# Modulation in four wide pairs with four products interleaved, its later two thirds moved beside w_pw and w_out, and GpSimd taken out of the first stage

## The chip, the cores and the metric

The kernel runs on one core of one Trainium2 chip. The metric is device time in microseconds (us), the median of three runs. Engines are named as in the profile: PE is TensorE (PEld its weight loads), DVE is VectorE, ACT is ScalarE, POOL is GpSimd and SP is SyncE, which issues all of the kernel's DMAs here.

## What is computed

Two transformer blocks on 512 tokens of width 1024, in float32. Only the first half of the first block matters here:

```python
mod = jnp.einsum("bd,de->be", jax.nn.silu(c), w_ada[l]) + b_ada[l]
sh1, sc1, g1, sh2, sc2, g2 = jnp.split(mod[:, None, :], N_MOD, axis=-1)
h = rms_norm(x, norm_mix_g[l]) * (1.0 + sc1) + sh1
proj = jnp.einsum("bsd,de->bse", h, w_in[l]) + b_in[l]
...
a = glu_in[..., :CONV_WIDTH] * jax.nn.sigmoid(glu_in[..., CONV_WIDTH:])
a = causal_depthwise_conv(a, conv_dw_w[l], conv_dw_b[l])
a = jax.nn.silu(layer_norm(a, conv_ln_g[l], conv_ln_b[l]))
y_conv = jnp.einsum("bsc,cd->bsd", a, w_conv_pw[l]) + b_conv_pw[l]
...
y = jnp.einsum("bsd,de->bse", g_conv * y_conv + g_mlstm * y_mlstm, w_out[l])
x = x + g1 * y
h = rms_norm(x, norm_ffn_g[l]) * (1.0 + sc2) + sh2
...
x = x + g2 * jnp.einsum("bsf,fd->bsd", jax.nn.silu(gt) * up, w_ffn_down[l])
```

The depthwise convolution has 31 taps per channel. `w_ada` is 1024 by 6144: 24 MB of weights for one vector times matrix. Of its six outputs the first two (`sh1`, `sc1`) are wanted before the first projection, `g1` first after `w_out`, `sh2` and `sc2` before the feed-forward, `g2` after it.

## The kernel before

Activations lie transposed, channels on the partitions: eight tiles of 128 channels by 512 tokens. A projection works by output tiles of 128 channels, with eight k tiles of 128. Each weight and each activation is cut into a high and a low part, and one k tile costs three products of 128x128 by 128x512: weight high and weight low times activation high (L1295, L1296), weight high times activation low (L1303). An output tile is so 24 products.

`plan()` writes one list of steps; each engine then runs, in that order, the part of each step that is its own. So a step that is added stands in the same place in every engine's queue, and an engine that waits holds back all that stands behind it.

Weight tiles come in over SP into a ring of four raw buffers (`load`). `split` makes the high part on ACT (L1446) and the low part on the engine `lo_engine` (POOL, L2245, until the convolution gate; DVE, L1694, after it) into a ring of three. `W["ahead"]` says how many units are cut in advance of the one that is finished.

Spare DVE work is handed out between products: `between()` is called three times per output tile, and `rate` says how many items of `spare` go into DVE's queue each time. In the opening six chunks of `w_ada`, 1 MB each and 256 outputs wide, are loaded. For the first eight chunks DVE takes five of the eight k tiles (`mod_near`, L1724, L1728), ACT three (`mod_far`, L1466) and POOL adds these (L2256, L2258); PE sums over the partitions with a column of ones (L1336), and DVE and ACT make the normed and shifted activations (`mod_tiles`), while two output tiles are interleaved k by k (`gemms`). The other sixteen chunks are 128 DVE items (`ada`, L1769, L1773) handed out in the GLU projection, at 3 per call. Behind them come the taps of the convolution: seven channel tiles on DVE (`tap`, L1791, L1794), pairs of tiles alternating, and the eighth on POOL (`tap_far`, L2270 to L2276).

The order of the work around the change is: the GLU projection (16 output tiles), `w_v` (two blocks of 96 products, in four banks at once), the gates `w_if`, q and k of four heads (16 tiles, each with three taps of a short convolution on DVE, L1860), each head's attention as side work (`attend`: scores L1363, values L1371, transposes L1377), 16 gate tiles, then `conv_sum(7)` and its product L1382, the 8 tiles of the convolution gate with the layer norm beside them, `w_pw`, `w_out`, and the first feed-forward. `w_pw` has three DVE operations per tile (L1920, L1923, L1925, with ACT's L1557 between the last two), `w_out` has one and a sum (L1930, L1700).

Of the kernel before, what the change touches and what calls it, by code (L numbers as in the profile page):

```python
# [7 lines left out]
ALU = mybir.AluOpType  # L8
# [32 lines left out]
GMIX, GFFN = 8, 80  # L41
SCALE = 1.0 / float(np.sqrt(96.0))
# [57 lines left out]
def plan():  # L100
# [25 lines left out]
    W = {"cut": 0, "used": 0, "finished": 0, "ahead": 2, "loaded": 0}  # L126
    lo_engine = ["pool"]
# [27 lines left out]
    far, side, spare, later_ops = [], [], [], []  # L155
    rate, due, tick = [0, 0, 0], [0.0, 0.0], [0]
# [17 lines left out]
    def between():  # L174
        while later_ops and later_ops[0][0] <= tick[0]:
            later_ops.pop(0)[1]()
        tick[0] += 1
        step(rate[0])
        due[0] += rate[1]
        background(int(due[0]))  # L180
        due[0] -= int(due[0])
        due[1] += rate[2]
        while due[1] >= 1:
            due[1] -= 1
            if far:
                far.pop(0)()
# [48 lines left out]
    def gemms(jobs, acts, together=2, hook=None, feed=None):  # L235
# [15 lines left out]
        ready("dve")  # L251
# [107 lines left out]
    order = [0, 4, 1, 5, 2, 6, 3, 7] + list(range(8, 24))  # L359
    place = {ch: n for n, ch in enumerate(order)}  # L360

    def ada_load(n, after=()):
        add("ada_load", n, order[n], after)

    for n in range(6):
        ada_load(n)
    for _ in range(NRAW - 1):
        load()
    csil = keepc(8)
    add("csil", csil)  # L370
    ss, other = SumSq("x0a"), SumSq("x0b")
    for i in range(8):
        if i % 2:
            other.add(("XT", i), [("x", 0, i)], eng="pool")
        else:
            ss.add(("XT", i), [("x", 0, i)])
    add("merge", ss.a, other.a, ss.t, other.t)
    tmp.give(other.a, ("merged",))
    ss.t = ("merged",)
    b0 = rows_of(ss, D)  # L380
    mod_a, mod_b, mod_c = misc.take(), misc.take(), misc.take()
    turns, turn_free = [mod_a[0], mod_c[0]], [mod_a[1], mod_c[1]]
    gmix = keepc(8)

    def mod_sums(p):
        chs, accs = (p, p + 4), [tmp.take(), tmp.take()]
        more = []
        for z, ch in enumerate(chs):
            more.append(tmp.take())
            add("mod_far", ch, place[ch] % 6, more[z], accs[z])  # L390
        for k in range(5):
            for z, ch in enumerate(chs):
                add("mod_near", ch, place[ch] % 6, k, accs[z])
        for z, ch in enumerate(chs):
            add("mod_sum", ch, accs[z][0], more[z][0], turns[p % 2], turn_free[p % 2])
            tmp.give(more[z][0], ("mod_sum", ch))
            tmp.give(accs[z][0], ("mod_cols", ch))
            ada_load(place[ch] + 6, [("mod_sum", ch)])

    def mod_tiles(p):  # L400
        add("mod_tiles", p, turns[p % 2])
        turn_free[p % 2] = [("mod", p)]

    mod_sums(0)
    add("xn", b0)
    misc.give(b0, ("xn", 7))
    mod_sums(1)
    load()

    def mod_feed(k):  # L410
# [11 lines left out]
    ada_acc = {}

    def ada_part(ch, k):
        if k == 0:
            ada_acc[ch] = tmp.take()
        add("ada", ch, place[ch] % 6, k, ada_acc[ch])
        if k == 7 and place[ch] + 6 < 24:
            ada_load(place[ch] + 6, [("ada", ch, 7)])
# [16 lines left out]
    def glu(i):  # L446
# [14 lines left out]
        def then():  # L461
            if i % 2:
                taps.extend(sums)
                sums.clear()
                if i < 7:
                    sums.append(lambda: conv_sum(i))
                taps.extend([lambda z=z, j=j: add("tap", i - 1 + z, j)
                             for j in range(31) for z in range(2) if i - 1 + z < 7])
# [3 lines left out]
    taps, sums, waiting = [], [], []  # L472
    for ch in range(8, 24, 2):
        parts = [lambda k=k, c=c: ada_part(c, k) for k in range(8) for c in (ch, ch + 1)]
        spare.extend(parts[:6] + waiting + parts[6:])
        waiting = [lambda ch=ch: (ada_columns(ch), ada_columns(ch + 1))]
    rate[:] = [0, 3, 0]
    gemms([job for i in range(8) for job in glu(i)], "n1", feed=mod_feed)
    background(1000)
    spare.extend(taps)  # L480
    far.extend([lambda j=j: add("tap_far", j) for j in range(31)])

    def last_columns():
        yield
        ada_columns(22)
        ada_columns(23)
        add("modb", mod_b[0])
        misc.give(mod_b[0], ("modb",))

    side.append(last_columns())  # L490
    rate[:] = [1, 3.5, 0.3]

# [100 lines left out]
    rate[:] = [1, 1.35, 0.3]  # L593
# [19 lines left out]
    rate[:] = [1, 1.6, 0.3]  # L613
    for n, (first, i) in enumerate([(32, i) for i in range(6)] + [(48, i) for i in range(6)] +
                                   [(32, 6), (32, 7), (48, 6), (48, 7)]):
        if n == 8:
            rate[1] = 2.1
# [4 lines left out]
    while far:  # L622
        far.pop(0)()
# [34 lines left out]
    rate[:] = [1, 0, 0]  # L658
    lo_engine[0] = "dve"
# [16 lines left out]
    gemms([("w_pw", i, pw_evac(i), None) for i in range(8)], "a")  # L676
    rate[:] = [0, 0, 0]
# [9 lines left out]
    gemms([("w_out", i, out_evac(i), None) for i in range(8)], "z", 0)  # L687
# [5 lines left out]
    def ffn_up(which, acts, names, hook=None):  # L693
# [100 lines left out]
    rate[:] = [1, 0, 0]  # L794
# [270 lines left out]
def program(nc, A, out, known):  # L1065
    steps, units = plan()
    ctx = ExitStack()
    with ctx:
# [27 lines left out]
        TRIG = place("trig", o, [128, 4, S]); o += 4128  # L1096
        HT = place("htok", o, [128, 4, 258]); o += 4128
# [15 lines left out]
        ADA = [place(f"ada{i}", B + 33728 + 8192 * i, [128, 8, 256]) for i in range(6)]  # L1113
# [32 lines left out]
        XN = CO  # L1146
# [71 lines left out]
        def _(e):  # L1218
# [59 lines left out]
            run({"begin": begin, "load": load, "ada_load": ada_load, "v_begin": v_begin, "rot_load": rot_load,  # L1278
# [4 lines left out]
        def _(e):  # L1283
# [1173 lines left out]
```

## Time and profile before

| | us |
|---|---|
| median of 3 runs | 1799.83 (1798.41 to 1801.11) |
| the profiled execution | 1799.9 |
| its span, first to last instruction | 1797.8 |
| PE busy in the span | 1623.5 |
| DVE busy | 1100.4 |
| ACT busy | 641.2 |
| POOL busy | 413.9 |

Busy shares are means over stages with different limits: PE is busy in 90% of the span, DVE in 61%, but DVE in nearly all of the first 540 us. 2.1 us of the execution lie outside the span. Starts in the rows are in us from the span's start; some records of matmuls are missing from the trace.

### The profile page before, as it was taken

Reading aid. Unit: us, or ns where it says so; the run is one execution under the profiler, and the core shown is the slowest. Engines: PE = TensorE matmul, PEld = TensorE weight load, DVE = VectorE, ACT = ScalarE, POOL = GpSimd, SP = SyncE. Lnnn points to the kernel's source line nnn. Section 1 sums busy time; section 2 is a strip of 40 time slices with the busy share of each in tenths; the row PEclk is TensorE's granted clock in tenths of the full one; section 3 lists DMA queues with packets and bytes.
Section 4 is the critical chain, followed back from the end, with each engine's and each line's share of the span. In section 5 each row is a group of like instructions: output and inputs, shape, how many; then the busy total and the mean of one; then the engine's idle time right before and its main releaser. Section 6 shows DMA issues by size and latency. Waiting matters only on the chain.

```text
span 1797.8 us, 18431 instructions
## 1 busy us (share of the span) xinstructions
PE 1623.5 (90%) x7112; PEld 1310.5 (73%) x7112; DVE 1100.4 (61%) x1538; ACT 641.2 (36%) x917; POOL 413.9 (23%) x242
## 2 busy tenths in 40 slices
PE   2898768778857998999999999899997999999988
PEld 2787656556746787888888888677885888888876
DVE  6889798899995455333337344866647444443246
ACT  4321135554416334223223322344634322322223
POOL 4445654556731001000001100100024111110010
PEclk9899889889988998999999999999999999999999
DMA  8672211111222332333333332221132333333332
GB/s 327 233 278 97 59 47 48 47 55 51 68 61 59 95 105 71 94 100 99 94 94 97 89 114 73 69 69 49 36 117 94 94 96 104 94 88 97 97 117 70
DMA packets 44734, 172.86 MB, mean 96 GB/s; under 512 B 4964, under 2 KB 5092, under 8 KB 41320
## 3 DMA queue, kind: packets, MB, share of 16 engines
q1 hardware_dynamic: 44648, 171.69, 30.2%
q8 instruction: 56, 0.92, 0.2%
q14 instruction: 30, 0.25, 0.0%
HBM read 167.48 MB, written 4.19 MB: 95 GB/s over the span
## 4 chain that ended last, share of the span: by engine, by line
PE 63%; DVE 13%; ACT 3%; issue 2%; POOL 0%; DVEq 0%; ACTq 0%; POOLq 0%
PE bank L1295 19%; PE bank L1296 19%; PE bank L1303 19%; DVE convout L1794 5%; PE bank L1388 1%; PE bank L1401 1%; DVE hm L1906 1%; PE bank L1331 1%; DVE XT L2183 1%; DVE tmp L1860 1%; PE bank L1315 1%; DVE spl L1694 0%; PE bank L1317 0%; DVE tmp L2180 0%; PE bank L1316 0%
## 5 line engine op out<-in xcount | busy, mean ns | idle before, releaser
L1295 PE MATMUL bank<-HH,sph 128*128 128x512 f32 x1496 | 608.9, 407 | 17.0 <-ACT HH L1665 5.2
L1296 PE MATMUL bank<-HH,spl 128*128 128x512 f32 x1496 | 594.9, 398 | 0.0
L1694 DVE TENSOR_TENSOR spl<-raw,sph 128x1024 fp32r<-128x1024 f32 (+1 forms) x207 | 265.6, 1286 | 334.4 <-ACT sph L1446 334.2
L1303 PE MATMUL bank<-HL,sph 128*128 128x512 f32 x1496 | 392.3, 398 | 1.1 <-DVE HL L2187 1.1
L1446 ACT ACTIVATE sph<-raw 128x1024 fp32r<-128x1024 f32 (+1 forms) x263 | 271.4, 1034 | 241.9 <-PE bank L1303 173.8
L1295 PEld LDWEIGHTS bank<-HH,sph 128*128 128x128 f32 x1496 | 289.0, 193 | 88.0 <-issue 16.4
L1296 PEld LDWEIGHTS bank<-HH,spl 128*128 128x128 f32 x1496 | 288.9, 193 | 62.0 <-issue 2.2
L1303 PEld LDWEIGHTS bank<-HL,sph 128*128 128x128 f32 x1496 | 284.3, 191 | 65.2 <-DVE HL L2187 2.9
L1794 DVE SCALAR_TENSOR_TENSOR convout<-convin,vecs,convout 128x512 f32<-128x512 f32 x210 | 215.5, 1074 | 0.9
L2245 POOL TENSOR_TENSOR spl<-raw,sph 128x1024 fp32r<-128x1024 f32 x56 | 165.2, 2954 | 175.3 <-ACT sph L1446 175.3
L2251 POOL TENSOR_TENSOR tmp<-tmp,tmp 128x512 f32<-128x512 f32 x44 | 60.1, 1372 | 555.4 <-ACT tmp L1454 554.7
L1295 PE MATMUL bank<-midh,sph 128*128 128x512 f32 x352 | 138.7, 394 | 0.0
L1296 PE MATMUL bank<-midh,spl 128*128 128x512 f32 x352 | 138.7, 394 | 0.0
L1585 ACT ACTIVATE midh<-tmp 128x512 fp32r<-128x512 f32 x44 | 27.8, 632 | 192.9 <-DVE tmp L1975 97.8
L1303 PE MATMUL bank<-midl,sph 128*128 128x512 f32 x352 | 89.9, 394 | 0.0
L1303 PEld LDWEIGHTS bank<-midl,sph 128*128 128x128 f32 x352 | 65.8, 187 | 16.3
L1295 PEld LDWEIGHTS bank<-midh,sph 128*128 128x128 f32 x352 | 65.8, 187 | 16.3
L1296 PEld LDWEIGHTS bank<-midh,spl 128*128 128x128 f32 x352 | 65.8, 187 | 16.3
L2305 POOL TENSOR_TENSOR midl<-tmp,midh 128x512 fp32r<-128x512 f32 x22 | 28.4, 1293 | 206.9 <-ACT midh L1585 206.9
L1773 DVE SCALAR_TENSOR_TENSOR tmp<-ada,kept,tmp 128x256 f32<-128x256 f32 x112 | 67.8, 673 | 0.0
L1860 DVE SCALAR_TENSOR_TENSOR tmp<-xpad,vecs,tmp 128x512 f32<-128x512 f32 x48 | 57.5, 1198 | 3.3 <-ACT tmp L1504 2.0
L2274 POOL TENSOR_SCALAR rrow<-convin,vecs 128x512 f32<-128x512 f32 x30 | 59.0, 1967 | 0.0
(287 smaller groups left out, 1707.6 us busy)
## 6 DMA issues: line engine op xcount, KB each, us to landing
raw<-in_w_in SPq DMA_DIRECT2D x73, 512.0 KB, 3.6
raw<-in_w_up SPq DMA_DIRECT2D x66, 512.0 KB, 3.6
ada<-in_w_ada SPq DMA_DIRECT2D x24, 1024.0 KB, 7.5
raw<-in_w_down SPq DMA_DIRECT2D x32, 512.0 KB, 3.5
raw<-in_w_gate SPq DMA_DIRECT2D x22, 512.0 KB, 3.6
raw<-in_w_down SPq DMA_DIRECT2D x16, 384.0 KB, 3.1
raw<-in_w_v SPq DMA_DIRECT2D x8, 512.0 KB, 3.7
raw<-in_w_pw SPq DMA_DIRECT2D x8, 512.0 KB, 3.6
```

The costliest lines, as they stand in the source:

```text
L1295: e.matmul(P_[b][:], sph(n)[:, q], hi[:, k, :], start=k == 0, stop=False)
L1296: e.matmul(P_[b][:], spl(n)[:, q], hi[:, k, :], start=False, stop=False)
L1303: m = e.matmul(P_[b][:], sph(n)[:, q], low[:, k, :], start=False, stop=last and k == kb - 1)
L1446: e.activation(sph(n), raw(n), ACT.Copy).then_inc(*up("s_w_high", ("wh", n)))
L1694: e.tensor_tensor(spl(n), raw(n), sph(n).bitcast(F32), ALU.subtract).then_inc(*up("s_w_low", ("wl", n)))
L1773: e.scalar_tensor_tensor(wide, x[:, k, :], KEEP[:, k:k + 1], wide, ALU.mult, ALU.add).then_inc(*up("s_ada", ("ada", ch, k)))
L1794: ins = e.scalar_tensor_tensor(CO[:, i, :], src, wt, CO[:, i, :], ALU.mult, ALU.add)
L1860: e.scalar_tensor_tensor(TMP[j][:], XP[:, s, k:k + 512], wt, TMP[j][:], ALU.mult, ALU.add).then_inc(*up("s_qk_conv", ("qk_conv", h, z, k)))
L2245: e.tensor_tensor(spl(n), raw(n), sph(n).bitcast(F32), ALU.subtract).then_inc(*up("s_w_low_p", ("wl", n)))
L2251: e.tensor_tensor(TMP[a][:], TMP[a][:], TMP[j][:], ALU.add).then_inc(*up("s_sum_p", ("ss", name, i)))
L2274: e.tensor_scalar(RROW[:], src, wt, None, ALU.mult).then_inc(*up("s_conv_p", ("tap_mul", j)))
L2305: e.tensor_tensor(ML[:, i, :], TMP[j][:], MH[:, i, :].bitcast(F32), ALU.subtract).then_inc(*up("s_cut_p", ("lo", "m2", i)))
```

## The change

The opening loads the first third of `w_ada` as four pairs (256 outputs of `sh1` and 256 of `sc1`, 512 wide) of four 512 KB transfers each, all into buffers of their own, with the first four weight tiles between them. For each pair DVE takes six of the eight k tiles in one chain, and PE takes the last two in the same accumulation as the sums over partitions: 12 matmuls per pair. The norm and the cut are now those of the later norms (`norm`, `normlo`), with both low parts on DVE. Four output tiles are interleaved instead of two, with a fourth slot of high and low parts for the opening alone. The later two thirds of `w_ada` come as 32 rows of 128x1024 (512 KB), two buffers, one DVE operation each, two per tile of `w_pw`, two per tile in the first half of `w_out`, one per tile in the first eight of the feed-forward; after every eighth, PE makes eight columns and DVE adds the bias. POOL has no `split`, no sum, no tap in the first stage; all eight channel tiles' taps are DVE's, at new rates. The diff, cut to its core:

```diff
-    W = {"cut": 0, "used": 0, "finished": 0, "ahead": 2, "loaded": 0}
-    lo_engine = ["pool"]
+    W = {"cut": 0, "used": 0, "finished": 0, "ahead": 4, "loaded": 0}
+    lo_engine = ["dve"]
...
-        ready("dve")
+        if together == 2:
+            ready("dve")
...
+    mod_a, mod_b, mod_c = misc.take(), misc.take(), misc.take()
+    for p in range(4):
+        add("ada_load", p)
+        if p < 2:
+            load()
+            load()
...
+    def mod_pair(p):
+        turn = (mod_a[0], mod_c[0])[p % 2]
+        acc = tmp.take()
+        add("mod_sum", p, acc, turn, turn_free[p % 2])
+        tmp.give(acc[0], ("mod_cols", p))
+        add("mod_tiles", p, turn)
         turn_free[p % 2] = [("mod", p)]
+        js = [tmp.take() for _ in range(2)]
+        for z in range(2):
+            add("norm", "n1", 2 * p + z, *js[z], b0, [])
+        for z in range(2):
+            add("normlo", "n1", 2 * p + z, js[z][0])
+            tmp.give(js[z][0], ("hi", "n1", 2 * p + z), ("lo", "n1", 2 * p + z))
+
+    mod_pair(0)
 
     def mod_feed(k):
+        if k in (0, 2, 4):
+            mod_pair(k // 2 + 1)
...
+    def ada_more(count):
+
+        for _ in range(count):
+            u = ada_at[0]
+            ada_at[0] += 1
+            add("ada", u)
+            if u + 2 < 32:
+                add("ada_more", u + 2)
+            if u % 8 == 7:
+                b, free = misc.take()
+                add("ada_columns", u // 8, b, free)
+                misc.give(b, ("modb", u // 8))
...
+                spare.extend([lambda z=z, j=j: add("tap", i - 1 + z, j)
+                             for j in range(31) for z in range(2)])
...
-    rate[:] = [0, 3, 0]
-    gemms([job for i in range(8) for job in glu(i)], "n1", feed=mod_feed)
+    rate[:] = [0, 2]
+    gemms([job for i in range(8) for job in glu(i)], "n1", 4, feed=mod_feed)
...
-    rate[:] = [1, 3.5, 0.3]
+    rate[:] = [1, 2.5]
...
-    rate[:] = [1, 1.35, 0.3]
+    rate[:] = [1, 1.2]
...
-    rate[:] = [1, 1.6, 0.3]
+    rate[:] = [1, 1.65]
...
-    gemms([("w_pw", i, pw_evac(i), None) for i in range(8)], "a")
+    add("ada_more", 0)
+    add("ada_more", 1)
+    gemms([("w_pw", i, pw_evac(i), lambda: ada_more(2)) for i in range(8)], "a")
...
-    gemms([("w_out", i, out_evac(i), None) for i in range(8)], "z", 0)
+    gemms([("w_out", i, out_evac(i), lambda: ada_more(2 if ada_at[0] < 24 else 0)) for i in range(8)], "z", 0)
...
+        if which == 1:
+            jobs = [(*job[:3], lambda: ada_more(1 if ada_at[0] < 32 else 0)) for job in jobs]
...
+            def ada_more(u):
+                if u < 2:
+                    w.wait_ge(*fenced("pw"))
+                else:
+                    w.wait_ge(at("ada", u - 2))
+                e.dma_start(MORE[u % 2][:], A["w_ada2"][u]).then_inc(*up(f"d_more{u % 2}", ("more", u), by=16))
...
+            def mod_sum(p, acc, b, free):
+                w.wait_ge(at("csil"), at("ones"), at("ada_w", p, 3), *each(free))
+                for z in range(4):
+                    et = 2 * p + z % 2 + 8 * (z // 2)
+                    column = P_[b][:, et:et + 1]
+                    for k in (0, 1):
+                        e.matmul(column, ADA[4 * p + 3][:, k, token(z)], KEEP[:, 6 + k:7 + k], start=k == 0, stop=False)
+                    w.wait_ge(at("mod_near", p, 5))
+                    m = e.matmul(column, TMP[acc[0]][:, token(z)], ONES[:, 0:1], start=False, stop=True)
+                m.then_inc(*up("s_column", ("mod_cols", p)))
+
+            def ada_columns(cb, b, free):
+                w.wait_ge(at("ada", 8 * cb + 7), at("ones"), *each(free))
+                for i in range(8):
+                    m = e.matmul(P_[b][:, i:i + 1], ACC[:, token(i)], ONES[:, 0:1], start=True, stop=True)
+                m.then_inc(*up("s_column", ("ada_cols", cb)))
...
+            def ada(u):
+                k, s = u % 8, KEEP[:, u % 8:u % 8 + 1]
+                w.wait_ge(at("more", u))
                 if k == 0:
+                    if u:
+                        w.wait_ge(at("ada_cols", u // 8 - 1))
+                    else:
+                        w.wait_ge(*fenced("pw"))
+                    ins = e.tensor_scalar(ACC[:], MORE[u % 2][:], s, None, ALU.mult)
                 else:
+                    w.wait_ge(at("ada", u - 1))
+                    ins = e.scalar_tensor_tensor(ACC[:], MORE[u % 2][:], s, ACC[:], ALU.mult, ALU.add)
```

## Rows read from the trace of the kernel before

**Rows 1.** The page's chain that ended last, shares by engine
```profile
PE 63%; DVE 13%; ACT 3%; issue 2%; POOL 0%; DVEq 0%; ACTq 0%; POOLq 0%
```

**Rows 2.** Busy time by stretch: PE, PEld, DVE, ACT, POOL, granted clock, DMA share, GB/s
```profile
70.00:152.00 82.00, 81.65 (x388) 68.23 (x387) 77.07 (x131) 19.74 (x23) 39.22 (x13) 1.00 0.62 224
152.00:222.00 70.00, 55.62 (x227) 44.49 (x226) 59.19 (x73) 10.42 (x11) 47.12 (x19) 0.88 0.24 73
222.00:407.00 185.00, 142.21 (x559) 108.26 (x558) 167.60 (x218) 94.31 (x138) 96.65 (x50) 0.88 0.17 50
407.00:521.00 114.00, 103.54 (x439) 82.44 (x437) 107.15 (x127) 48.42 (x69) 79.85 (x37) 0.96 0.24 70
521.00:544.00 23.00, 0.16 (x1) 0.00 (x0) 22.15 (x32) 1.40 (x2) 0.00 (x0) 0.61 0.00 0
```

**Rows 3.** What PE waited for, 152 to 545 us: total, times, longest
```profile
PE bank L1377 <- DVE htok L1901: 24.4, 4, 8.0
PE bank L1382 <- DVE tmp L1805: 22.8, 1, 22.8
PE bank L1351 <- DVE row L1850: 12.8, 1, 12.8
```

**Rows 4.** DVE's groups by shape, 222 to 407 us: busy, mean ns
```profile
L1794 DVE SCALAR_TENSOR_TENSOR convout<-convin,vecs,convout 128x512 f32<-128x512 f32 x72 | 69.2, 1005 | 0.0
L1860 DVE SCALAR_TENSOR_TENSOR tmp<-xpad,vecs,tmp 128x512 f32<-128x512 f32 x48 | 57.5, 1198 | 3.3 <-ACT tmp L1504 2.0
```

**Rows 5.** The taps in 522 to 542 us, where POOL is idle
```profile
L1794 DVE SCALAR_TENSOR_TENSOR convout<-convin,vecs,convout 128x512 f32<-128x512 f32 x24 | 18.0, 751 | 0.7
```

**Rows 6.** DVE's timeline (start, us): alternating taps; short taps; POOL idle
```profile
258.85 2.73 DVE L1794 SCALAR_TENSOR_TENSOR convout<-convin,vecs,convout 128x512 f32<-128x512 f32 x4
...
343.40 2.33 DVE L1860 SCALAR_TENSOR_TENSOR tmp<-xpad,vecs,tmp 128x512 f32<-128x512 f32 x3
```

**Rows 7.** DVE's groups, 150 to 156 us: modulation 256 wide, POOL nearly idle
```profile
L1773 DVE SCALAR_TENSOR_TENSOR tmp<-ada,kept,tmp 128x256 f32<-128x256 f32 x12 | 4.9, 475 | 0.0
```

**Rows 8.** Timeline of the opening: the norm's last DVE step; PE's eight column passes (four matmuls)
```profile
18.78 0.87 DVE L1717 TENSOR_SCALAR tmp<-consts,small 128x128 f32<-128x128 f32 x4
...
57.67 1.20 PE L1336 MATMUL bank<-ones,tmp 128*128 128x1 f32 x8 [2.47 <-DVE tmp L1733]
```

**Rows 9.** ACT's timeline: first operations after certain output tiles
```profile
151.78 0.69 ACT L1476 ACTIVATE tmp<-bank,vecs 128x512 f32<-128x512 f32 x1 [5.22 <-PE bank L1303]
...
228.53 0.69 ACT L1501 ACTIVATE xpad<-bank,vecs 128x512 f32<-128x512 f32 x1
...
407.36 0.69 ACT L1537 ACTIVATE tmp<-bank,vecs 128x512 f32<-128x512 f32 x1
...
721.38 0.60 ACT L1577 ACTIVATE tmp<-bank 128x512 f32<-128x512 f32 x1 [3.13 <-PE bank L1303]
...
732.26 0.60 ACT L1577 ACTIVATE tmp<-bank 128x512 f32<-128x512 f32 x1 [3.14 <-PE bank L1303]
```

**Rows 10.** DVE's timeline in w_pw: the first operation of five tiles
```profile
609.27 0.75 DVE L1920 SCALAR_TENSOR_TENSOR tmp<-bank,vecs,gconv 128x512 f32<-128x512 f32 x1
...
612.05 0.75 DVE L1920 SCALAR_TENSOR_TENSOR tmp<-bank,vecs,gconv 128x512 f32<-128x512 f32 x1
...
619.10 0.74 DVE L1920 SCALAR_TENSOR_TENSOR tmp<-bank,vecs,gconv 128x512 f32<-128x512 f32 x1
...
623.36 0.75 DVE L1920 SCALAR_TENSOR_TENSOR tmp<-bank,vecs,gconv 128x512 f32<-128x512 f32 x1
...
639.68 0.75 DVE L1920 SCALAR_TENSOR_TENSOR tmp<-bank,vecs,gconv 128x512 f32<-128x512 f32 x1 [1.25 <-PE bank L1303]
```

**Rows 11.** Busy time by stretch around one wait of PE, columns as above
```profile
368.30:376.60 8.30, 0.32 (x2) 0.00 (x0) 7.75 (x25) 3.96 (x6) 2.24 (x2) 0.75 0.16 56
376.60:382.70 6.10, 6.09 (x19) 5.12 (x20) 6.03 (x6) 2.04 (x3) 5.52 (x2) 0.50 0.15 32
```

**Rows 12.** The page's DMA issues: KB each, us to landing
```profile
raw<-in_w_pw SPq DMA_DIRECT2D x8, 512.0 KB, 3.6
```

More of the change, by code:

```diff
@@ L358, in plan @@
     add("begin")
[L359 to L369, printed above, removed]
+    mod_a, mod_b, mod_c = misc.take(), misc.take(), misc.take()
[4 more added lines that the diff above has]
+            load()
+    csil, gmix = keepc(8), keepc(8)
@@ L370, in plan @@
     add("csil", csil)
-    ss, other = SumSq("x0a"), SumSq("x0b")
+    ss = SumSq("x0")
     for i in range(8):
[L373 to L379, printed above, removed]
-    b0 = rows_of(ss, D)
-    mod_a, mod_b, mod_c = misc.take(), misc.take(), misc.take()
-    turns, turn_free = [mod_a[0], mod_c[0]], [mod_a[1], mod_c[1]]
@@ L383, in plan @@
[L383 to L398, printed above, removed]
@@ L417, in mod_feed @@
+    mod_pair(0)
+    def mod_feed(k):
+        if k in (0, 2, 4):
+            mod_pair(k // 2 + 1)
         if k == 6:
             W["ahead"] = NSPL
+            misc.give(b0, ("norm", "n1", 7))
             misc.give(mod_a[0], *turn_free[0])
             misc.give(mod_c[0], *turn_free[1])
[L422 to L429, printed above, removed]
@@ L436, in plan @@
+    ada_at = [0]
     total = {}
@@ L462, in then @@
             if i % 2:
-                taps.extend(sums)
+                spare.extend(sums)
                 sums.clear()
@@ L466, in then @@
                     sums.append(lambda: conv_sum(i))
-                taps.extend([lambda z=z, j=j: add("tap", i - 1 + z, j)
-                             for j in range(31) for z in range(2) if i - 1 + z < 7])
+                spare.extend([lambda z=z, j=j: add("tap", i - 1 + z, j)
+                             for j in range(31) for z in range(2)])
         return [("w_in", i, keep, None), ("w_in", 8 + i, evac, then)]
[L472 to L476, printed above, removed]
-    rate[:] = [0, 3, 0]
-    gemms([job for i in range(8) for job in glu(i)], "n1", feed=mod_feed)
[L479 to L490, printed above, removed]
-    rate[:] = [1, 3.5, 0.3]
+    sums = []
+    rate[:] = [0, 2]
+    gemms([job for i in range(8) for job in glu(i)], "n1", 4, feed=mod_feed)
+    rate[:] = [1, 2.5]
     fence("v")
@@ L1112, in program @@
         SEL = place("sel", B + 88064, [4, 4, 128])
-        ADA = [place(f"ada{i}", B + 33728 + 8192 * i, [128, 8, 256]) for i in range(6)]
+        ADA = [place(f"ada{i}", B + 17344 + 4096 * i, [128, 2, 512]) for i in range(16)]
         IR, LF, BR, CR = [place(f"row{i}", B + 50176 + 2048 * i, [4, S]) for i in range(4)]
@@ L1700, in total @@
                     e.tensor_tensor(TMP[a][:], TMP[a][:], TMP[j][:], ALU.add).then_inc(*up("s_sum", ("ss", name, i)))
-            def merge(a, b, after, other):
-                w.wait_ge(at(*after), at(*other))
-                e.tensor_tensor(TMP[a][:], TMP[a][:], TMP[b][:], ALU.add).then_inc(*up("s_sum", ("merged",)))
             def rsqrt(name, src, v, q, r, n, scale, after):
@@ L1781, in glu, with ada_columns @@
+            def ada_columns(cb, b, free):
+                part = slice(16 + 8 * cb, 24 + 8 * cb)
+                w.wait_ge(at("ada_cols", cb), at("vecs"))
+                e.tensor_tensor(MOD[:, part], P_[b][:, 0:8], V_[:, VEC["b_ada"] + 16 + 8 * cb:VEC["b_ada"] + 24 + 8 * cb],
+                                ALU.add).then_inc(*up("s_ada", ("modb", cb)))
             def glu(i, b, g, v, j, free):
```

216 lines of the change are left out of this document (69 added, 147 removed).

## Prediction

> **What bounds the kernel now.** I read the page's chain first: PE sets 63% of the end, DVE 13% [rows 1]. The stretches say where DVE does. From 222 to 407 us (q, k and attention) DVE is busy 167.6 of 185 us, from 407 to 521 (gates) 107.2 of 114, and from 521 to 544 PE stands and DVE is busy 22.2 of 23 [rows 2]. The waits give the reason: PE waits 22.8 us for the sum over the convolution's tiles, because DVE is still busy with taps, and 24.4 and 12.8 us for other DVE results [rows 3]. Next come the durations. Beside POOL a tap takes 1005 ns and a short tap 1198 [rows 4]; with POOL idle a tap takes 751 [rows 5], four that alternate between two tiles take 2.73 us, so one each 0.66, and three short ones 2.33, so 0.78 [rows 6]. So the first 540 us are paced by a DVE that POOL slows, and what follows mostly by PE: a feed-forward pair of tiles takes 732.26 - 721.38 = 10.88 us [rows 9], 5.44 per tile, 0.227 per product.
>
> **The opening and the GLU projection.** Its last gate stands at 151.8 us [rows 9]. Removed: ACT's and POOL's share of the modulation, and POOL's sums. Added: per pair one chain on one engine after the other. Six 512-wide operations at 0.78 (the dependent kind) are 4.4 us with the cheaper first. Then PE's columns: 12 matmuls in two passes each, four of the passes early, leave 20; eight take 1.20 us [rows 8], so 3.0 at full clock and up to twice that. Then two small DVE operations, two norms and two low parts, some 4 us. About 12.5 us per pair, and DVE stands during the columns. With four low parts of weights (1.2 each) after the first pair, and a start near 18 us (the norm's last step ends at 19.65 now [rows 8], after a merge with POOL's sum that goes), the pairs end near 31, 48, 61 and 74 us, and the 96 interleaved products near 83. The four products per k tile fill PE's waits, but the next weights' slots come free only then: ACT's table, two sigmoids and a high part, then DVE's low part hold PE for some 5 us more and cost it clock. Twelve tiles are left. DVE per tile: six taps 4.0, a low part 1.15, half a GLU 0.4, together 5.5, as much as PE's 5.44: 66 us, so about 157. **+5** (0 to +12). The loads cost nothing: they are issued at the start, the second pair's weights some 30 us before use, on an SP that now waits for nobody there. POOL's queue holds nothing more before the layer norm, so nobody waits for it.
>
> **w_v and w_if up to the first q tile**: 228.5 - 151.8 = 76.7 us now [rows 9]. 240 products are 54.4. DVE has 47 taps (31 us), ten low parts (11.5) and the adds (5.4): 48, less than PE. With 4 to 5 for the banks that wait: 59. **-18** (-12 to -21).
>
> **q, k and attention**: 407.4 - 228.5 = 178.8 us [rows 9]. DVE's 167.6 [rows 2] are 72 taps and their starts (73), 48 short taps (57.5) [rows 4] and 37 of the rest. After: 57 taps at 0.66 and the starts (38), short taps at 0.78 (37), the rest without POOL some 30, and 16 low parts that were POOL's (18): 124, plus some 12 in which DVE waits for exponentials. So 136 is the lower bound. PE's own work is 16 tiles (87) and three heads (some 11 each): 120, but it must still wait for DVE at each head's values and transposes, and each wait lets the clock fall. The other bound is nearly no gain, because the low parts now stand behind taps in DVE's queue. I take 38 us per head where it is now some 44, and 41 for the first: 155. **-24** (-8 to -38).
>
> **Gates up to the sum's product**: 407.4 to 544.0, 136.6 us [rows 2, 9]. PE: 16 tiles 87, one head 13, waits 6: 106. DVE: 72 taps 48, 16 low parts 18, 16 products 11, the head 12: 89, so no backlog of taps is left and the 22.8 us go [rows 3]. **-30** (-20 to -35). The new rates hand out 72 + 47 + 57 + 79 = 255 items for 251, so none is left over. Sum so far **-67**.
>
> **The later modulation.** 32 operations, 1024 wide. The trace has 475 ns at 256 [rows 7] and 751 at 512 [rows 5]: 276 more per 256, so an estimate of 1.28 each, 2.6 per pair. The Trainium skill, "VectorE: DVE Perf Modes", section "The TRN2 errata", gives (N + 151)/0.96 ns for a float32 tensor_tensor, 1.22 us here; by that the 24 operations up to w_out would be 1.4 us shorter and the result 1788.
>
> In w_pw a tile's three operations take 612.05 - 609.27 = 2.78 us, with the low part 623.36 - 619.10 = 4.26 [rows 10]. Count from 609.27. DVE: tile 0 to 2.8, two operations (one cheaper) to 4.9, tile 1 to 7.7, 10.3, tile 2 13.1, 15.7, tile 3 with its low part 20.0, 22.6. Only then is the eighth operation done, and PE's columns, which stand in PE's queue before tile 4's products, wait for it. PE has ended tile 3 at 639.68 - 4 x 5.44 = 617.9, which is 8.7: it stands 14 us. Eight column matmuls are 16 passes, 2.4 us [rows 8], 3.6 at a fallen clock: 26.2. Tile 4 takes 5.44 + 2.3, since a stretch after a wait of 8 us ran 6.1 us at 0.50 [rows 11]: 33.9. DVE again, 2.78 or 4.26 plus 2.6 each: 59.9 after tile 7, where PE has stood 9.7 us; columns to 63.5. Before, PE was there at 30.4 [rows 10]. **+33**.
>
> In w_out DVE has 4.26 less one operation (0.69), plus 2.6: 6.2 per tile for four tiles. Tile 0 ends at 71.2, the eighth operation at 94.7, PE stood 7 us, columns to 98.3, four tiles and 2.3 to 122.4. Before, 30.4 + 43.5 = 73.9: 48.5 in all, so **+15** here. In the feed-forward DVE has slack but for the last columns: 3.5 of waiting, 2.4, and 2 of clock, **+8**. The 32 transfers: 512 KB land in 3.6 us [rows 12], and some 4 lie between a buffer's use and its next; hidden, barely. On SP the raw loads stand behind them, but a raw tile is wanted four tiles later. If they come late it is 1 us per tile, +10. Without any loss of clock 12 less. **+56** (44 to 66).
>
> The profiled execution took 1799.9 us, 2.1 more than its span and as much as the median 1799.83. 1799.9 - 67 + 56 = **1789**.
>
> **Rivals.** *The bottom goes out of the waits:* DVE, no longer slowed, is never late for PE between 152 and 545 us, so that the 60 us of waits [rows 3] shrink to a tenth and the clock stays up: 15 more gained than the 67, 82, so 1774. For it: DVE's content falls by a quarter. Against: these waits are chains through ACT and DVE, not only lateness. *Slower:* the low parts in DVE's queue hold PE. DVE's queue is in order, and the low part of a tile stands behind the taps of two tiles and a head's scores, which wait for ACT; POOL had no such queue. If that leaves 6 us in q and k, 18 in the gates, 12 in w_v, with +10 at the opening, 26 are gained for 56: 1830. It decides from the point where the first half gains less than 56. *The clock stays low:* PE fell to 0.50 after a wait of 8 us [rows 11] but stands at 1.00 from 70 to 152, where it is busy throughout [rows 2]. If DVE's pace leaves a small wait in each of the 12 GLU tiles and the clock stays at 1.2 GHz in them, a tile takes 10.2 instead of 5.5: 56 more, 1845. The Trainium skill, "TensorE: Matmul & The Clock Gate", section "HAM oscillation", describes such a loop, where every burst begins cold after its wait. In rows 2 short waits of a tile don't show that, so it has a small chance. *The moved modulation is hidden:* only columns and a few us are paid, 13 instead of 56: 1746. Against it: PE's columns wait for DVE in both queues' order.
>
> **How the numbers follow.** 1789 (own range 1778 to 1800) 0.42, of it 0.29 faster, 0.11 same, 0.02 slower; 1774: 0.22; 1830: 0.24; 1845: 0.05; 1746: 0.07. What a measurement of this kernel can tell from no change is about 0.2%, 3.6 us. Faster 0.29 + 0.22 + 0.07 = 0.58, same 0.11, slower 0.31. A range of 1766 to 1830 leaves out the hidden case, the low clock and a little beyond.
>
> **What would show it.** Right: taps at 0.66 to 0.75 us throughout, no wait of 20 us before the sum's product, that product near 477, and three PE waits of 14, 10 and 7 us before columns in w_pw and w_out, with w_out's end 48 us later after the w_pw group than now. Wrong: PE waits for low parts (L1694's successor) in q and k, a product of the sum after 500, or no waits at the columns.

## The result, and the profile after

The changed kernel takes **1757.3 us** (median of 4 runs, 1756.7 to 1758.6) against 1799.1 (4 runs) for the kernel before: ratio 0.9767, 95% interval 0.975 to 0.9784, so 42 us faster. The forecast was 11 us faster, 1789, and the range ended at 1766. The direction was right; the time lies 9 us below the range. The profiled execution took 1756.8 us, its span is 1755.0, again about 2 less.

The chain of work that ended last, by engine [rows 1]:

```profile
PE 66%; DVE 8%; ACT 4%; issue 1%; DMA 1%; POOL 0%; DVEq 0%; ACTq 0%; POOLq 0%
```

DVE's share falls from 13% to 8%. Where the span is cut as in the prediction, ACT's first operation of each part now starts here (timeline, start in us) [rows 9]:

```profile
149.15 0.69 ACT L1446 ACTIVATE tmp<-bank,vecs 128x512 f32<-128x512 f32 x1 [4.32 <-PE bank L1282]
...
207.94 0.69 ACT L1471 ACTIVATE xpad<-bank,vecs 128x512 f32<-128x512 f32 x1
...
346.29 0.69 ACT L1507 ACTIVATE tmp<-bank,vecs 128x512 f32<-128x512 f32 x1
```

The stretches between those points, with the columns of [rows 2]:

```profile
70.00:149.00 79.00, 75.81 (x327) 62.16 (x327) 65.84 (x91) 18.67 (x21) 0.00 (x0) 0.98 0.29 89
149.00:208.00 59.00, 57.13 (x250) 46.31 (x249) 49.08 (x68) 17.07 (x19) 0.24 (x2) 1.00 0.31 96
208.00:346.00 138.00, 124.38 (x530) 95.48 (x529) 119.31 (x218) 87.94 (x130) 0.09 (x1) 0.99 0.22 65
346.00:447.00 101.00, 99.34 (x440) 80.41 (x439) 89.54 (x159) 50.21 (x71) 0.00 (x0) 1.00 0.28 84
```

In q, k and attention DVE has 119.3 us of work where it had 167.6, and the clock of PE is 0.99 where it was 0.88. The gates are PE's: busy 99.3 of 101 us. The stretch in which PE stood for 23 us before the sum's product is gone. DVE's groups by shape in 208 to 346 us [rows 4]:

```profile
L1747 DVE SCALAR_TENSOR_TENSOR convout<-convin,vecs,convout 128x512 f32<-128x512 f32 x59 | 42.3, 744 | 0.0
L1813 DVE SCALAR_TENSOR_TENSOR tmp<-xpad,vecs,tmp 128x512 f32<-128x512 f32 x48 | 36.0, 750 | 2.7 <-ACT tmp L1474 1.4
L1664 DVE TENSOR_TENSOR spl<-raw,sph 128x1024 fp32r<-128x1024 f32 x17 | 20.7, 1218 | 0.0
```

A tap takes 744 ns where it took 1005, a short tap 750 where it took 1198. PE's waits in 149 to 447 us (total, times, longest) [rows 3]:

```profile
PE bank L1274 <- DVE spl L1664: 6.0, 2, 3.6
PE bank L1360 <- DVE htok L1854: 4.8, 3, 1.7
PE bank L1354 <- DVE sc L1824: 2.7, 3, 1.3
PE bank L1334 <- DVE row L1803: 1.1, 1, 1.1
```

The waits for transposes' inputs fall from 24.4 to 4.8 us, the one for the gates' row from 12.8 to 1.1, and the 22.8 for the sum over the convolution is no longer in the list. The new price stands later. PE's largest wait in 440 to 720 us is the one for the accumulator of the moved modulation (`modacc`):

```profile
PE bank L1327 <- DVE modacc L1725: 33.0, 4, 15.2
```

PE's timeline, first around the end of the 96 interleaved products, then around the first columns in `w_pw`:

```profile
78.39 0.40 PE L1282 MATMUL bank<-HL,sph_first 128*128 128x512 f32 x1
81.97 0.47 PE L1274 MATMUL bank<-HH,sph 128*128 128x512 f32 x1 [3.19 <-DVE spl L1664]
...
535.93 3.57 PE L1327 MATMUL bank<-ones,modacc 128*128 128x1 f32 x16 [15.17 <-DVE modacc L1725]
539.37 0.77 PE L1274 MATMUL bank<-ah,sph 128*128 128x512 f32 x1
```

`w_pw` and `w_out` as one stretch, the kernel before in the first fence, the kernel after in the second:

```profile
609.00:683.00 74.00, 74.00 (x324) 60.35 (x322) 42.35 (x51) 21.84 (x28) 0.00 (x0) 1.00 0.33 101
```

```profile
513.00:635.00 122.00, 91.55 (x370) 75.11 (x368) 70.01 (x78) 21.82 (x28) 0.00 (x0) 0.82 0.54 167
```

What took 74 us takes 122: PE stands 30.5 of them, and its busy time is 17.5 longer, at a clock of 0.82. Three groups of columns at 3.57 us, as in the timeline, are 10.7 of that. For the transfers DVE waits only 2.6 us here.

All runs are compared by such stretches. Each is the time between the same events: last GLU gate, first q tile, first gate tile, product of the convolution's sum, first `w_pw` tile, last `w_out` tile, first tile of the feed-forward's second product, end.

| us | opening, GLU | w_v, w_if | q, k, attention | gates | conv gate, norm | w_pw, w_out | feed-forward | rest | median |
|---|---|---|---|---|---|---|---|---|---|
| before | 151.8 | 76.7 | 178.8 | 136.6 | 65.3 | 73.9 | 267.3 | 847.3 | 1799.1 |
| after | 149.1 | 58.8 | 138.4 | 100.3 | 66.2 | 121.4 | 276.0 | 844.8 | 1757.3 |
| pool_low_parts | 150.4 | 74.2 | 154.8 | 109.8 | 65.9 | 120.9 | 274.5 | 849.5 | 1801.9 |
| pool_reads_beside | 172.2 | 89.8 | 185.6 | 135.6 | 67.0 | 118.8 | 275.5 | 844.9 | 1891.5 |
| pool_writes_beside | 151.0 | 59.1 | 144.5 | 102.4 | 65.6 | 120.0 | 274.6 | 849.4 | 1763.1 |
| before_without_pool | 149.6 | 64.8 | 144.4 | 124.2 | 65.8 | 73.9 | 266.0 | 844.1 | 1736.7 |
| before_moved_only | 144.4 | 82.5 | 172.1 | 116.7 | 63.9 | 120.7 | 274.6 | 849.6 | 1826.2 |
| two_interleaved | 153.5 | 58.8 | 138.4 | 100.3 | 64.3 | 119.8 | 274.5 | 849.6 | 1759.8 |
| columns_later | 149.2 | 58.8 | 138.3 | 100.3 | 63.9 | 89.4 | 269.0 | 848.7 | 1720.2 |
| modulation_from_gate | 148.9 | 58.8 | 138.4 | 100.3 | 65.9 | 77.7 | 273.5 | 846.7 | 1712.6 |

So the first four stretches gave 97.4 us and the moved modulation took 56.2 (47.5 and 8.7). The prediction had 67 and 56. The other two stretches, the convolution gate and the rest, change by 0.9 and -2.5.

### The profile page after: what moved, and what is told of

Its sections match the earlier page's. It is cut to its first block, busy times and chain, and to the rows that moved or that the text cites. A ratio compares the mean times of both kernels' runs of the same rounds, so it can differ in the third digit from the quotient of the medians.

```text
span 1755.0 us, 18373 instructions
## 1 busy us (share of the span) xinstructions
PE 1624.6 (93%) x7176; PEld 1317.9 (75%) x7176; DVE 1016.9 (58%) x1507; ACT 632.0 (36%) x893; POOL 124.6 (7%) x102
## 3 DMA queue, kind: packets, MB, share of 16 engines
q1 hardware_dynamic: 48104, 171.70, 31.2%
## 4 chain that ended last, share of the span: by engine, by line
PE 66%; DVE 8%; ACT 4%; issue 1%; DMA 1%; POOL 0%; DVEq 0%; ACTq 0%; POOLq 0%
PE bank L1274 20%; PE bank L1275 20%; PE bank L1282 19%; DVE modacc L1725 1%; DMA more<-in_w_ada 1%; DVE spl L1664 1%; PE bank L1371 1%; PE bank L1327 1%; PE bank L1384 1%; PE bank L1310 1%; DVE XT L2141 1%; ACT tmp L1437 1%; DVE tmp L2138 0%; PE bank L1294 0%; PE bank L1296 0%
## 5 line engine op out<-in xcount | busy, mean ns | idle before, releaser
L1664 DVE TENSOR_TENSOR spl<-raw,sph 128x1024 fp32r<-128x1024 f32 (+1 forms) x262 | 332.3, 1271 | 333.1 <-ACT sph L1429 332.7
L1282 PE MATMUL bank<-HL,sph 128*128 128x512 f32 x1488 | 387.9, 395 | 1.1 <-DVE HL L2145 1.1
L1282 PEld LDWEIGHTS bank<-HL,sph 128*128 128x128 f32 x1488 | 280.0, 189 | 64.2 <-DVE HL L2145 2.8
L1747 DVE SCALAR_TENSOR_TENSOR convout<-convin,vecs,convout 128x512 f32<-128x512 f32 x240 | 167.1, 744 | 0.0
L2208 POOL TENSOR_TENSOR tmp<-tmp,tmp 128x512 f32<-128x512 f32 x41 | 55.7, 1365 | 552.4 <-ACT tmp L1437 551.9
L1275 PEld LDWEIGHTS bank<-midh,spl 128*128 128x128 f32 x352 | 65.8, 187 | 16.3
L1282 PEld LDWEIGHTS bank<-midl,sph 128*128 128x128 f32 x352 | 65.8, 187 | 16.3
L1274 PEld LDWEIGHTS bank<-midh,sph 128*128 128x128 f32 x352 | 65.8, 187 | 16.3
L1933 DVE TENSOR_TENSOR tmp<-tmp,bank 128x512 f32<-128x512 f32 x22 | 15.1, 687 | 52.7 <-PE bank L1282 52.7
L1327 PE MATMUL bank<-ones,modacc 128*128 128x1 f32 x64 | 14.3, 353 | 33.0 <-DVE modacc L1725 33.0
L1437 ACT ACTIVATE tmp<-XT 128x512 f32<-128x512 f32 x32 | 19.4, 620 | 59.1 <-DVE XT L1883 54.9
L1327 PEld LDWEIGHTS bank<-ones,modacc 128*128 128x128 f32 x64 | 13.9, 330 | 34.7 <-DVE modacc L1725 34.7
```

The costliest lines, as they stand in the source:

```text
L1274: e.matmul(P_[b][:], sph(n)[:, q], hi[:, k, :], start=k == 0, stop=False)
L1275: e.matmul(P_[b][:], spl(n)[:, q], hi[:, k, :], start=False, stop=False)
L1282: m = e.matmul(P_[b][:], sph(n)[:, q], low[:, k, :], start=False, stop=last and k == kb - 1)
L1327: m = e.matmul(P_[b][:, i:i + 1], ACC[:, token(i)], ONES[:, 0:1], start=True, stop=True)
L1437: e.activation(TMP[j][:], source(src), ACT.Square, scale=vec(*scale) if scale else 1.0).then_inc(*up("s_square", ("sq", name, i)))
L1664: e.tensor_tensor(spl(n), raw(n), sph(n).bitcast(F32), ALU.subtract).then_inc(*up("s_w_low", ("wl", n)))
```

## The experiments

**Low parts back on POOL, nothing else.** The changed kernel, with POOL cutting the low parts from the end of the interleaved group to the convolution gate:

```diff
             W["ahead"] = NSPL
+            lo_engine[0] = "pool"
...
+    lo_engine[0] = "dve"
     side.append(layer_norm())
```

> The changed kernel with one part undone: from the fifth weight tile up to the convolution gate the low parts of the weights are POOL's again; taps and all else stay on DVE. If POOL's presence slows DVE (taps 0.74 us in the changed kernel, 1.0 in the kernel before), taps and short taps rise to 0.85 us or more and the 56 us of low parts that DVE loses are given back: about 1760 to 1790. If POOL only mattered by work done or not done, DVE has 56 us less and the kernel is not slower than 1757. If the slow low part itself (2.95 us) is what PE waited for, PE's waits for POOL's low parts appear by name, and the taps stay at 0.74.

Measured: 1801.9 us, ratio to the kernel before 1.0023 (1.0011 to 1.0036). That is 12 us more than the highest time expected. This one part undone gives back the whole gain; 41 us of it lie in the three stretches from the last GLU gate to the sum's product. DVE's groups in 210 to 490 us and POOL's one large group:

```profile
L1749 DVE SCALAR_TENSOR_TENSOR convout<-convin,vecs,convout 128x512 f32<-128x512 f32 x138 | 132.6, 1010 | 0.0
L1815 DVE SCALAR_TENSOR_TENSOR tmp<-xpad,vecs,tmp 128x512 f32<-128x512 f32 x48 | 54.1, 1127 | 3.9 <-ACT tmp L1476 2.6
...
L2204 POOL TENSOR_TENSOR spl<-raw,sph 128x1024 fp32r<-128x1024 f32 x33 | 87.8, 2664 | 178.4 <-ACT sph L1431 178.4
```

POOL is busy in a third of the time and the mean tap is back at 1010 ns. PE's waits in 149 to 490 us:

```profile
PE bank L1362 <- DVE htok L1856: 12.5, 4, 4.5
PE bank L1336 <- DVE row L1805: 8.8, 1, 8.8
...
PE bank L1296 <- POOL spl L2204: 2.5, 1, 2.5
```

DVE is rid of 33 low parts of 1.22 us, PE waits for POOL's slow one only once, 2.5 us, and yet the waits for DVE at the heads come back, 12.5 us of the 24.4 for the transposes' inputs and 8.8 of the 12.8 for the row. So it isn't the low part's place in a queue that costs, but what POOL's operation does to DVE's. The timeline shows it on single operations, DVE's in the first fence, POOL's in the second:

```profile
228.19 2.50 DVE L1782 TENSOR_TENSOR_SCAN row<-tmp,row 4x128 f32<-4x128 f32 x1 [0.33 <-POOL kept L2220]
...
232.28 0.41 DVE L1782 TENSOR_TENSOR_SCAN row<-tmp,row 4x128 f32<-4x128 f32 x1
...
239.93 2.44 DVE L1787 TENSOR_TENSOR_SCAN mrow<-row,kept 4x128 f32<-4x128 f32 x1
```

```profile
228.02 2.39 POOL L2204 TENSOR_TENSOR spl<-raw,sph 128x1024 fp32r<-128x1024 f32 x1
...
239.70 2.39 POOL L2204 TENSOR_TENSOR spl<-raw,sph 128x1024 fp32r<-128x1024 f32 x1 [9.29 <-ACT sph L1431]
```

A scan of 0.41 us, started 0.17 us after POOL's low part, takes 2.50 and ends 0.28 us after it (228.02 + 2.39 = 230.41; 228.19 + 2.50 = 230.69). The other scan ends 0.28 after its low part too (242.09 and 242.37). In these two places DVE isn't slowed, it stands until POOL is done. The Trainium skill, "SBUF — State Buffer", section "Who interferes with whom", says that a DVE instruction with two SBUF inputs contends with a GpSimd instruction that reads SBUF, not with one that only writes it, through an exclusive lock. These two operations agree with that; the next two runs test the two halves of the rule.

**POOL reads, POOL writes, for nobody.** The changed kernel, and on POOL, for each of the weight units 8 to 56, work that nobody waits for: four additions that read two SBUF operands, or ten memsets. (What they write is never read.)

```diff
+                if 8 <= n < 57:
+                    w.wait_ge(at("wh", n), at("vecs"))
+                    for r in range(4):
+                        if n > 8 or r:
+                            w.wait_ge(at("beside", 4 * n + r - 1))
+                        e.tensor_tensor(RROW[:], V_[:, 0:512], V_[:, 0:512], ALU.add).then_inc(
+                            *up("s_beside", ("beside", 4 * n + r)))
```

```diff
+                if 8 <= n < 57:
+                    w.wait_ge(at("wh", n))
+                    for r in range(10):
+                        if n > 8 or r:
+                            w.wait_ge(at("beside", 10 * n + r - 1))
+                        e.memset(RROW[:], 0.0).then_inc(*up("s_beside", ("beside", 10 * n + r)))
```

> The changed kernel plus work that nobody waits for: at each of 49 weight tiles of the first stage POOL makes four additions of 128x512 from a constant tile into a tile that is not read, some 1.4 us each. If two engines reading at once is what slows DVE, taps rise towards 1.0 us, PE's waits at each head come back, the sum's product moves from 446 us to 490 or later, and the kernel takes 1795 or more. If lateness came from the order of the queues or from DVE's amount of work alone, nothing changes: 1757.

> As the run with POOL's additions, but POOL only writes: ten memsets of 128x512 at each of the 49 weight tiles. If the shared reading is what slows DVE, taps stay at 0.74 us and the kernel at 1757. If any work on POOL slows DVE, taps rise as with the additions.

Measured: with the reads 1891.5 us, 1.0524 (1.0507 to 1.0542) of the kernel before; with the writes 1763.1, 0.98 (0.978 to 0.9819). DVE's and POOL's groups with the reads (180 to 583 us), and then PE's waits in the same stretch:

```profile
L1747 DVE SCALAR_TENSOR_TENSOR convout<-convin,vecs,convout 128x512 f32<-128x512 f32 x177 | 188.4, 1105 | 0.0
L1664 DVE TENSOR_TENSOR spl<-raw,sph 128x1024 fp32r<-128x1024 f32 x42 | 71.2, 1696 | 1.0 <-ACT sph L1429 1.0
...
L2209 POOL TENSOR_TENSOR rrow<-vecs 128x512 f32<-128x512 f32 x156 | 219.7, 1408 | 162.0 <-ACT sph L1429 150.4
```

```profile
PE bank L1360 <- DVE htok L1854: 23.4, 4, 6.5
PE bank L1274 <- DVE spl L1664: 21.7, 7, 9.6
```

And with the writes (151 to 457 us):

```profile
L1747 DVE SCALAR_TENSOR_TENSOR convout<-convin,vecs,convout 128x512 f32<-128x512 f32 x177 | 123.8, 741 | 0.0
...
L2209 POOL MEMSET rrow<- 128x512 f32 x402 | 212.3, 528 | 82.3 <-ACT sph L1429 58.9
```

POOL is busy some 215 us either way. Reading, it makes a tap 1105 ns and the kernel 134 us slower than the change; writing, it leaves the tap at 741 and costs 6 us. The waits for transposes' inputs are back at 23.4 us, where they were 24.4 [rows 3], in a kernel whose order of work is the changed one. (The other waits are not those of before: 21.7 us are for low parts, and 2.3 for the row.) So those waits were DVE's lateness, made by POOL's reads.

What the writes cost lies for the most part in q, k and attention (6.2 us in the profiled execution), and there it is mostly the experiment's own. The first head takes 39.6 us instead of 34.1, the other three differ by 0.6 or less. DVE's first scan there needs two small memsets of POOL's, and these now stand behind the ten that nobody waits for. In the changed kernel, then with the writes:

```profile
210.55 0.41 DVE L1780 TENSOR_TENSOR_SCAN row<-tmp,row 4x128 f32<-4x128 f32 x1 [0.43 <-POOL kept L2218]
...
222.82 0.89 DVE L1799 TENSOR_SCALAR rowc<-rowc,row 4x128 f32<-4x128 f32 x3
```

```profile
216.96 0.41 DVE L1780 TENSOR_TENSOR_SCAN row<-tmp,row 4x128 f32<-4x128 f32 x1 [4.68 <-POOL kept L2224]
...
229.32 1.71 DVE L1799 TENSOR_SCALAR rowc<-rowc,row 4x128 f32<-4x128 f32 x3
```

DVE stands 4.3 us longer. Another 1.3 come from the copies and `tensor_scalar` operations a little later, which take longer beside the memsets (3.67 us for the series instead of 2.40). So writes are not free for every DVE operation; they are for the taps.

**The kernel before without POOL.** Opening, modulation beside the GLU projection and all later places as before; the low parts and the eighth tile's taps on DVE, at rates that hand them all out:

```diff
-    lo_engine = ["pool"]
+    lo_engine = ["dve"]
...
-                             for j in range(31) for z in range(2) if i - 1 + z < 7])
+                             for j in range(31) for z in range(2)])
...
-    far.extend([lambda j=j: add("tap_far", j) for j in range(31)])
...
-    rate[:] = [1, 1.6, 0.3]
+    rate[:] = [1, 2.05, 0.3]
...
-            rate[1] = 2.1
+            rate[1] = 2.95
...
```

> The kernel before with one part of the change alone: after the opening the first stage has nothing on POOL (low parts and the eighth tile's taps on DVE, tap rates raised so that none is left over); the opening and the later modulation beside the GLU projection stay. If POOL's presence was the cause, 40 to 60 us of the 98 that the first half gained appear although DVE keeps the 128 modulation items, and the kernel takes 1740 to 1765. If moving the modulation away made the first half faster, DVE is now overloaded by what POOL did and the kernel takes 1799 or more.

Measured: 1736.7 us, 0.9663 (0.9646 to 0.968), 3 below the range expected. These edits gain 62 us, 21 more than the whole change. DVE's taps and PE's largest wait in 150 to 483 us:

```profile
L1793 DVE SCALAR_TENSOR_TENSOR convout<-convin,vecs,convout 128x512 f32<-128x512 f32 x240 | 166.0, 744 | 0.0
```

```profile
PE bank L1294 <- DVE spl L1693: 18.0, 8, 3.9
```

DVE has more to do here (the modulation is still in the GLU projection, so taps run late into the gates, 124.2 us), and now PE does wait for low parts that stand behind taps, 18.0 us in eight waits. That was the prediction's slower rival; it exists, but where the first half carries the modulation, and at 18 us where 62 are gained.

**The move alone.** The kernel before with the later modulation in its new place and rates, POOL with low parts and taps as before:

```diff
...
-    rate[:] = [0, 3, 0]
...
+    rate[:] = [0, 2, 0]
...
-    gemms([("w_pw", i, pw_evac(i), None) for i in range(8)], "a")
...
+    gemms([("w_pw", i, pw_evac(i), lambda: ada_more(2)) for i in range(8)], "a")
...
```

> The kernel before with another part alone: the later modulation beside w_pw, w_out and the feed-forward as in the changed kernel, taps handed out from the GLU projection on at the changed kernel's rates; the opening, POOL's low parts and POOL's eighth tile of taps stay. If POOL's presence was the cause of the first half's gain, the first half gains 45 us or less against 56 us paid later: 1799 to 1815. If freeing DVE of 75 us of modulation was the cause, the first half gains 70 or more: 1785 or less.

Measured: 1826.2 us, 1.0154 (1.0127 to 1.0181): 26 us slower, and 11 above the range expected. The first five stretches get 29.6 us shorter, and 54 are paid in `w_pw`, `w_out` and the feed-forward. PE's waits for the heads in 144 to 516 us are still there:

```profile
PE bank L1380 <- DVE htok L1908: 22.9, 4, 6.3
PE bank L1354 <- DVE row L1857: 12.8, 1, 12.8
```

Fewer operations for DVE don't remove them; faster ones do. The 22.8 us before the sum's product are another matter: here they are gone too, with the gates at 116.7 us instead of 136.6, so that for this one wait fewer operations, at their new rates, are enough. POOL's absence (-62) and the move (+26) add to -36 of the -42. The other 6 are not taken apart: the new opening has no run of its own.

**Two tiles interleaved instead of four.** The changed kernel with `"n1", 2` for `"n1", 4` in the call of `gemms`:

```diff
-    gemms([job for i in range(8) for job in glu(i)], "n1", 4, feed=mod_feed)
+    gemms([job for i in range(8) for job in glu(i)], "n1", 2, feed=mod_feed)
```

> The changed kernel with two products interleaved in the opening instead of four, all else the same. If four fill PE's waits in the opening, the 96th product comes later than at 78.4 us and the kernel loses 5 to 9 us: 1762 to 1766. If the slots that come free together after the four (PE stands 3.6 us there) cost as much as the filling brings, it stays within 3 us of 1757.

Measured: 1759.8 us, 0.9782 (0.9758 to 0.9806), 2.5 above the change; the opening's stretch is 4.3 longer in the profile. The four products bring about that and not more.

**Columns two tiles later.** The changed kernel with an accumulator for each eight operations, and PE's columns put into the list two output tiles after their last operation:

```diff
-                b, free = misc.take()
-                add("ada_columns", u // 8, b, free)
-                misc.give(b, ("modb", u // 8))
+                columns_due.append([LATE, u // 8])
+        for entry in columns_due:
+            entry[0] -= 1
+        while columns_due and columns_due[0][0] < 0:
+            cb = columns_due.pop(0)[1]
+            b, free = misc.take()
+            add("ada_columns", cb, b, free)
+            misc.give(b, ("modb", cb))
...
-        ACC = place("modacc", o, [128, 1024])
+        ACC = [place(f"modacc{i}", B + 17344 + 4096 * i, [128, 1024]) for i in range(4)]
...
```

> The changed kernel with the columns of each eighth operation two tiles later in all queues and an accumulator of its own for each, so that PE does not stand for them. If PE's stand (33 us before four columns) and the clock lost with it are the price of the move, some 25 to 30 us go: 1727 to 1735. If DVE's amount of work in w_pw (6.9 us per tile against 5.4 of PE) is the price, PE waits for low parts instead and only 10 go: about 1747. If the transfers set the pace, DVE's waits for them stay and less than 5 go.

Measured: 1720.2 us, 0.9561 (0.954 to 0.9582), 37 below the change and better than expected. PE's waits in 440 to 720 us, where the change had 33.0 us for `modacc`, now begin with

```profile
PE bank L1280 <- DVE spl L1670: 5.6, 2, 4.0
PE bank L1309 <- DVE tmp L1676: 4.8, 2, 2.6
```

and hold none for it. `w_pw` and `w_out` take 89.4 us instead of 121.4, the feed-forward 269.0 instead of 276.0. The later place and the separate accumulators are one step here (with a single one DVE would wait for PE's columns before it begins the next eight); no run parts them.

**And begun in the convolution gate.** The same, with one of the 32 operations per tile from the convolution gate's eight tiles on, so that none comes twice in a tile:

```diff
+    add("ada_more", 0)
+    add("ada_more", 1)
...
+        ada_more(1)
...
-    gemms([("w_pw", i, pw_evac(i), lambda: ada_more(2)) for i in range(8)], "a")
+    gemms([("w_pw", i, pw_evac(i), lambda: ada_more(1)) for i in range(8)], "a")
...
-    gemms([("w_out", i, out_evac(i), lambda: ada_more(2 if ada_at[0] < 24 else 0)) for i in range(8)], "z", 0)
+    gemms([("w_out", i, out_evac(i), lambda: ada_more(1)) for i in range(8)], "z", 0)
...
+    for entry in columns_due:
+        entry[0] = 0
+    ada_more(0)
...
```

> As the run with later columns, and the modulation begins one stage earlier: one operation per tile of the convolution gate, w_pw, w_out and the first eight of the feed-forward. DVE is busy 27 of 63 us beside the convolution gate, so the move should now cost little more than the columns themselves, 4 times 2.4 us: 1710 to 1722. If DVE operations there delay the layer norm's chain, w_pw begins later by up to 10 us and the kernel stays above 1725.

Measured: 1712.6 us, 0.9526 (0.9504 to 0.9547), the fastest here. `w_pw` and `w_out`, the columns of [rows 2]:

```profile
512.00:590.00 78.00, 77.99 (x348) 63.66 (x346) 57.94 (x68) 21.84 (x28) 0.00 (x0) 1.00 0.58 192
```

PE stands nowhere in this stretch and its granted clock is 1.00; right behind it, where the third columns are queued at once, PE waits 3.4 us for them. The eight operations that went from here to the convolution gate can't be seen there: it takes 65.9 us, and 63.9 to 67.0 in the kernels without them. Against the kernel before without POOL, which keeps the modulation beside the GLU projection (1736.7), this one is 24 us faster: placed so, the move and the new opening together gain.

## Why the prediction was wrong in size

**The step that failed** is the term of q, k and attention: "but it must still wait for DVE at each head's values and transposes", with 38 us per head and 41 for the first, 155 in all, -24. It came to 138.4, -40.5: 16.5 us of the 32 by which the time was missed. By the starts of the first q tiles the heads took 34.1, 36.5, 31.2 and 36.6 us, where before they took 47.3, 42.8, 43.2 and 45.6. The prediction took the waits of [rows 3] for chains through ACT and DVE that a faster DVE leaves standing. The two runs with POOL's reads put back, which keep the changed order of work, bring the waits back at 12.5 and 23.4 us, against 4.8 without: they were lateness. The time came within 3 us of the "lower bound" of 136, which was worked out as DVE's own work (124 forecast, 119.3 measured) and a little waiting for ACT. The bound at -38 was too tight as well.

**Gates: -30 forecast, -36.4 measured**, in part for the same reason: the sum kept 6 us of waits, and 1.7 came; the 100 us that it had for the products and the head were 98.6. **The opening: +5 forecast, -2.6 measured**, a term that was mis-sized by 7.6 us. The four chains on DVE began at 18.0, 35.3, 47.7 and 58.1 us (forecast 18, then 31 and four low parts of 1.2, which is 35.8, then 48 and 61), the group ended at 78.8 instead of 83, and PE stood 3.2 us for the low part behind it (5 forecast). PE's columns held DVE for 4.5 us in the first two pairs but for 2.5 in the last two, so that the third and fourth took less than the 13 us of the sum. From the group's end to the last gate 70.4 us were measured; the prediction's 157 leaves 74 for it, though its own terms, 5 and 66, make 71. **`w_v` and `w_if`: -18 forecast, -18.0 measured.**

**The moved modulation was right: +56 forecast, +56.2 measured** (47.5 for `w_pw` and `w_out`, 8.7 in the feed-forward, forecast 48 and 8). Four waits for the columns, 15.2, 7.8, 6.7 and 3.4 us, against 14 + 9.7 + 7 + 3.5 = 34.2. (The 1.20 us of [rows 8] for eight passes, taken for full clock, stand at a granted clock of 0.82; sixteen took 1.84 us at 1.00 in the kernel with later columns. The sum used 3.6 for sixteen behind a wait, and 3.57 came.) One operation took 1282 ns (28 in 449 to 700 us); the estimate from rows of 256 and 512 was 1.28 us. The formula of the Trainium skill, "VectorE: DVE Perf Modes", section "The TRN2 errata", gives an estimate of 1.22, which is what the low part's tensor_tensor of the same width took (1218 ns), but not this scalar_tensor_tensor.

**The rivals.** "The bottom goes out of the waits" (1774, 0.22) named the right mechanism and still gave it 82 us where 97.4 came: it took no more than 15 us for the waits and the clock, and kept the +5 of the opening. The slower rival, low parts behind taps, cost 6.0 us in two waits here, both in q and k, where the prediction had named them as a sign against it. The clock that stays low in the GLU tiles did not come (0.98 in 70 to 149 us). The moved modulation wasn't hidden in this kernel; the last two runs show that it can nearly be, when PE's columns aren't put straight behind DVE's last operation.

Of the signs named ahead, taps at 0.74 us, no wait of 20 us before the sum's product and the waits at the columns came; the product itself came at 446.6 us, 30 before its forecast 477.

**What stays open.** The stretch "rest" runs from 844.1 to 849.6 us in kernels that are the same there; no run tells why. So the 2.5 us between four and two interleaved tiles can't be read from the whole time; the 4.3 in the opening can. What the new opening is worth by itself was not tested.

## What to carry to other kernels

Before GpSimd is given elementwise work beside a busy VectorE, compare the duration of VectorE's two-operand instructions in a stretch where GpSimd reads and in one where it is idle: here the work on the "free" engine cost 62 us more than the same work on VectorE. When such a slowdown goes, a wait behind the slowed engine should be priced by rerunning its queue at the new durations, not as a share of the old wait. And a step that makes one in-order engine use another's last result should be queued some tiles behind it; two tiles, with an accumulator for each group, were worth 37 us here.

## What the runs showed of the hardware that was not expected

- A POOL operation that reads two SBUF operands stopped a DVE operation with two SBUF operands until it ended: scans of 0.41 and 0.47 us took 2.50 and 2.44 us, and both ended 0.28 us after POOL's operation. With POOL busy a third of the time the mean tap went from 744 to 1010 ns.
- POOL's writes alone, 402 memsets of 528 ns, left the tap at 741 ns. They did lengthen operations on one tensor and a scalar: three `tensor_scalar` operations of 4x128 took 1.71 us beside them and 0.89 without.
- After the waits for columns PE ran at the lower of its two clock levels, 1.2 GHz. Behind the wait of 15.17 us, in the changed kernel:

```profile
535.90:543.00 7.10, 7.07 (x25) 6.29 (x26) 1.30 (x2) 0.00 (x0) 0.00 (x0) 0.50 0.55 168
```

Products were 0.43 us apart there instead of 0.23, and 16 column passes took 3.57 us where the kernel with later columns has

```profile
536.32 1.84 PE L1333 MATMUL bank<-ones,modacc 128*128 128x1 f32 x16
```

Of the 17.5 us of busy time that `w_pw` and `w_out` gained, 3 x 1.84 = 5.5 are so the columns at full clock and 12 the clock: a quarter of the 47.5.
